# The expert part's output rows: gathered, added by VectorE and scattered plainly, in place of an accumulating scatter

## The reference

```python
g_w, g_idx = lax.top_k(g_prob, 1)                      # one of 4 groups
e_logits = e_logits[jnp.arange(N), g_idx[:, 0]]        # its 8 experts
top_l, top_i = lax.top_k(e_logits, TOP_K_INNER)        # two of them
comb = g_w * jax.nn.softmax(top_l, axis=-1)
eid = g_idx * EXPERTS_PER_GROUP + top_i
...
def expert_block(args):
    xb, e = args
    return (jax.nn.silu(xb @ w_gate[e]) * (xb @ w_up[e])) @ w_down[e]
...
out = jnp.zeros((N, D), jnp.float32).at[stok].add(yp[dest].astype(jnp.float32) * sw[:, None])
# and in decoder_layer:
x = x + hier_moe(hn, ...)
```

## Time and profile before

| | us |
|---|---|
| median of 3 runs | 1002.82 |
| lowest, highest | 997.93, 1004.01 |
| span of the profiled execution | 995.0 |
| busy in it: PE / PEld / DVE / ACT / POOL | 876.9 / 482.7 / 377.6 / 218.1 / 94.0 |

### The profile page before, as it was taken

The page is one execution under the profiler, slowest core; times in us unless marked ns, Lnnn a source line. Parts: engine busy times, 40 slices in busy tenths (PEclk is TensorE's granted clock), DMA queues, the critical chain, the costliest instruction groups (busy, mean ns, idle before and its releaser), DMA issues.

```text
span 995.0 us, 11159 instructions
## 1 busy us (share of the span) xinstructions
PE 876.9 (88%) x4304; PEld 482.7 (49%) x4304; DVE 377.6 (38%) x841; ACT 218.1 (22%) x559; POOL 94.0 (9%) x104
## 2 busy tenths in 40 slices
PE   5999999999999999999969999787786868777774
PEld 4555777777688888745433333222232223222221
DVE  4689687786443445432635112111111111111010
ACT  3532645446332100021211111101010101011110
POOL 0100000000000000011011211101010101010111
PEclk9999999999999999999969999999889999899998
DMA  9621321121122229099289999999999999999994
GB/s 328 207 85 60 110 85 52 43 86 43 43 76 70 74 80 339 14 411 407 99 275 399 397 395 390 397 410 399 398 408 403 416 392 408 408 406 406 408 420 147
DMA packets 35925, 258.56 MB, mean 260 GB/s; under 512 B 9416, under 2 KB 12744, under 8 KB 20744
## 3 DMA queue, kind: packets, MB, share of 16 engines
q1 hardware_dynamic: 28912, 242.19, 61.3%
q0 software_dynamic: 6960, 15.65, 5.5%
HBM read 252.47 MB, written 14.58 MB: 268 GB/s over the span
## 4 chain that ended last, share of the span: by engine, by line
PE 77%; DVE 6%; DMA 6%; issue 6%; another core or an unknown queue 3%; ACT 1%; SPq 1%; POOL 0%; POOLq 0%; DVEq 0%; ACTq 0%
PE ps L1826 24%; PE ps L2111 20%; PE ps L2136 11%; PE ps L1764 6%; PE ps L1985 5%; DMA arena<-in_w_gu 5%; PE ps L2096 1%; PE ps L1911 1%; DMA arena<-in_x 1%; PE ps L1885 1%; PE ps L1842 1%; PE ps L1868 1%; PE ps L2019 1%; PE ps L2112 1%
## 5 line engine op out<-in xcount | busy, mean ns | idle before, releaser
L1826 PE MATMUL ps<-arena 128*128 128x272 f32 x1120 | 266.7, 394 | 2.6 <-DVE arena L1317 1.0
L2111 PE MATMUL ps<-arena 128*64 128x512 f32 x512 | 237.5, 612 | 32.1 <-DMA arena<-in_w_gu 31.2
L2112 PE MATMUL ps<-arena 128*64 128x512 f32 x512 | 237.9, 613 | 0.0
L1826 PEld LDWEIGHTS ps<-arena 128*128 128x128 f32 x1120 | 208.9, 190 | 52.3 <-issue 7.1
L2111 PEld LDWEIGHTS ps<-arena 128*64 128x64 f32 x512 | 67.5, 140 | 172.3 <-issue 137.6
L786 ACT ACTIVATE arena<-ps 128x272 f32<-128x272 f32 (+4 forms) x156 | 71.4, 465 | 345.1 <-PE ps L1826 168.4
L1616 DVE SCALAR_TENSOR_TENSOR arena<-arena,list_w,ps 64x512 f32<-64x512 f32 x32 | 24.0, 749 | 283.0 <-ACT arena L1043 283.0
L2136 PE MATMUL ps<-arena 128*64 128x512 f32 x256 | 67.9, 679 | 26.9 <-issue 26.1
L747 POOL DMA_INDIRECT out_y<-arena,list_i x32 | 45.6, 1426 | 385.8 <-DVE arena L1623 380.0
L2136 PE MATMUL ps<-arena,const 128*64 128x512 f32 x256 | 61.6, 625 | 21.5 <-issue 21.1
L1764 PE MATMUL ps<-arena 128*128 128x512 f32 (+1 forms) x192 | 74.0, 544 | 6.4 <-DVE arena L1109 6.4
(11 more groups left out here) (248 smaller groups left out, 719.8 us busy)
## 6 DMA issues: line engine op xcount, KB each, us to landing
arena<-in_w_gu SPq DMA_DIRECT2D x61, 2048.0 KB, 53.1
arena<-in_w_ed SPq DMA_DIRECT2D x30, 2048.0 KB, 53.5
arena<-in_w_pair SPq DMA_DIRECT2D x20, 1024.0 KB, 4.9
arena<-in_w_gu SPq DMA_DIRECT2D x12, 512.0 KB, 7.6
arena<-in_w_q SPq DMA_DIRECT2D x2, 2048.0 KB, 15.0
arena<-in_w_out SPq DMA_DIRECT2D x2, 2048.0 KB, 12.6
arena<-in_x SPq DMA_DIRECT2D x4, 512.0 KB, 10.0
arena<-in_w_ed SPq DMA_DIRECT2D x2, 1024.0 KB, 7.6
```

Of the source, the lines that this page charges most:

```text
L1826: ins = mm(out, w[:, k, :], tokens[:, k, :], start=k == 0 and q in "127", stop=k == 3, skip_group_check=q not in "127")
L2111: mm(ps[0:C, 2 + s, :], xT[s][:, j, :], w[:, jj, 1, :], start=j == 0, stop=j == JX - 1)
L2112: ins = mm(ps[64:64 + C, 2 + s, :], xT[s][:, j, :], w[:, jj, 0, :], start=j == 0, stop=j == JX - 1)
```

## The change

Each step's 64 rows of y are now gathered into y_rows[s] ahead of time (gather_y, an indirect DMA from y), VectorE adds the down product to both halves in place (add_base), and POOL scatters the sum back by an indirect DMA without compute_op (put_y). add_base waits for the new semaphores y_base[s] (the gathered rows) beside dn_ready. ScalarE's take_y is gone. POOL's loop is written anew: in iteration e it gathers x of e+3, waits until put_y(e-2), the last user of buffer e % 2, has landed, gathers y of e, waits for y_taken e and scatters y of e-1. y_taken is one semaphore now. VectorE's loop is unrolled into 32 straight steps. Overflow items keep the copy and the accumulating scatter (take_y on VectorE alone, add_y).

The diff, without the declarations of the semaphores and the constants of the loop:

```diff
+            def gather_y(index, s):
+                pool.indirect_dma_start(
+                    out=y_rows[s][0:C, :], out_offset=None, in_=o["y"],
+                    in_offset=bass.IndirectOffsetOnAxis(ap=index, axis=0),
+                    bounds_check=T - 1, oob_is_err=False).then_inc(y_base[s], 16)
+
+            def put_y(index, s):
+                pool.indirect_dma_start(
+                    out=o["y"], out_offset=bass.IndirectOffsetOnAxis(ap=index, axis=0),
+                    in_=y_rows[s][0:C, :], in_offset=None,
+                    bounds_check=T - 1, oob_is_err=False).then_inc(y_out[s], 16)
...
-            for e in range(2, NE + 4):
-                if e < NE:
-                    pool.wait_ge(xe_ready, e - 1)
-                    gather_x(list_i[:, e:e + 1], e % 2)
-                if e >= 4:
-                    for q in range(2):
-                        pool.wait_ge(y_taken[q], e - 3)
-                    above(pool, y_out[(e - 1) % 2], 16 * ((e - 3) // 2))
-                    add_y(list_i[:, e - 4:e - 3], e % 2)
+            for e in range(-1, NE + 1):
+                if e + 3 < NE:
+                    pool.wait_ge(xe_ready, e + 2)
+                    gather_x(list_i[:, e + 3:e + 4], (e + 3) % 2)
+                if 0 <= e < NE:
+                    above(pool, y_out[e % 2], 16 * (e // 2))
+                    gather_y(list_i[:, e:e + 1], e % 2)
+                if e > 0:
+                    pool.wait_ge(y_taken, e)
+                    put_y(list_i[:, e - 1:e], (e - 1) % 2)
...
-            def take_y(e, s, turn):
-
-                act.wait_ge(dn_ready, e + 1)
-                above(act, y_out[s], 16 * turn)
-                act.sem_inc(passed, 1)
-                copy(y_rows[s][0:C, 512:1024], ps[64:64 + C, 6 + s, :]).then_inc(y_taken[1], 1)
...
+            def add_base(e, s):
+
+                dve.wait_ge(dn_ready, e + 1)
+                dve.wait_ge(y_base[s], 16 * (e // 2 + 1))
+                dve.sem_inc(passed, 1)
+                tt(y_rows[s][0:C, 0:512], ps[0:C, 6 + s, :], y_rows[s][0:C, 0:512], ALU.add)
+                tt(y_rows[s][0:C, 512:1024], ps[64:64 + C, 6 + s, :], y_rows[s][0:C, 512:1024], ALU.add).then_inc(y_taken, 1)
+
...
-                dve.tensor_copy(y_rows[s][0:C, 0:512], ps[0:C, 6 + s, :]).then_inc(y_taken[0], 1)
...
+            def step(e):
+
+                s = e % 2
+                if e == NE - 1:
+                    add_base(e - 1, 1 - s)
+                hidden(e, s, list_w[0:C, 0, e:e + 1])
+                if e < NE - 1:
                     take_x(e + 1, 1 - s)
-                if not last and (not isinstance(e, int) or e > 0):
-                    take_y(e - 1, 1 - s, half - (1 - s))
+                if 0 < e < NE - 1:
+                    add_base(e - 1, 1 - s)
...
-            for k in range(1, 1 + UNROLL):
-                step(k, k, k // 2)
-            with dve.Fori(1, STEPS) as it:
-                for k in range(1, 1 + UNROLL):
-                    step(it * UNROLL + k, k, it * (UNROLL // 2) + k // 2)
-            step(NE - 1, 1, NE // 2 - 1, last=True)
-            take_y(NE - 1, 1, NE // 2 - 1)
+            for e in range(1, NE):
+                step(e)
+            add_base(NE - 1, 1)
...
-                for q in range(2):
-                    above(pe, y_taken[q], e - 1)
+                above(pe, y_taken, e - 1)
```

More of the change, by code:

```diff
@@ L50 @@
 N_CHUNK = 11
-UNROLL = 10
 MASKED = -1.0e30
@@ L376, in build @@
         dn_ready = sem("dn_ready")
-        y_taken = [sem("y_taken_dve"), sem("y_taken_act")]
+        y_taken = sem("y_taken")
+        y_base = [sem(f"y_base{s}") for s in range(2)]
         y_out = [sem(f"y_out{s}") for s in range(2)]
@@ L386, in build @@
         N_CONST = 6
-        STEPS = (NE - 2) // UNROLL
         def slot(n, *shape):
@@ L777, in _ @@
                     gather_x(item_list_i[:, :], 0)
-                    for q in range(2):
-                        pool.wait_ge(y_taken[q], i + (NE + 1))
-                        pool.sem_inc(passed, 1)
+                    pool.wait_ge(y_taken, i + (NE + 1))
+                    pool.sem_inc(passed, 1)
                     add_y(item_list_i[:, :], 0)
@@ L1058, in _ @@
                 take_hidT(e - 1, 1 - s)
-                if e == NE - 1:
-                    take_y(e - 1, 1 - s, (e - 1) // 2)
                 do_silu(e, s, root_of(e))
-                if e < NE - 1:
-                    take_y(e - 1, 1 - s, (e - 1) // 2)
             take_hidT(NE - 1, 1)
-            take_y(NE - 1, 1, NE // 2 - 1)
             act.wait_ge(item_ready, 1)
@@ L1073, in _ @@
                     take_hidT(i + NE, 0)
-                    take_y(i + NE, 0, i + NE // 2)
         @block.vector
@@ L1617, in hidden @@
                     .then_inc(hid_ready, 1)
+            def add_base(e, s):
[4 more added lines that the diff above has]
+                tt(y_rows[s][0:C, 512:1024], ps[64:64 + C, 6 + s, :], y_rows[s][0:C, 512:1024], ALU.add).then_inc(y_taken, 1)
             def take_y(e, s, turn):
                 dve.wait_ge(dn_ready, e + 1)
-                above(dve, y_out[s], 16 * turn)
+                dve.wait_ge(y_out[s], 16 * turn)
                 dve.sem_inc(passed, 1)
-                dve.tensor_copy(y_rows[s][0:C, 0:512], ps[0:C, 6 + s, :]).then_inc(y_taken[0], 1)
[L1625 to L1631, removed]
-                    take_y(e - 1, 1 - s, half - (1 - s))
-                hidden(e, s, column(list_w, e))
-                if not last:
+                dve.tensor_copy(y_rows[s][0:C, 0:512], ps[0:C, 6 + s, :])
+                dve.tensor_copy(y_rows[s][0:C, 512:1024], ps[64:64 + C, 6 + s, :]).then_inc(y_taken, 1)
+            def step(e):
[4 more added lines that the diff above has]
+                if e < NE - 1:
                     take_x(e + 1, 1 - s)
-                if not last and (not isinstance(e, int) or e > 0):
-                    take_y(e - 1, 1 - s, half - (1 - s))
+                if 0 < e < NE - 1:
+                    add_base(e - 1, 1 - s)
             def list_items():
@@ L1676, in _ @@
             take_x(0, 0)
-            step(0, 0, 0)
+            step(0)
             list_items()
-            for k in range(1, 1 + UNROLL):
-                step(k, k, k // 2)
-            with dve.Fori(1, STEPS) as it:
-                for k in range(1, 1 + UNROLL):
-                    step(it * UNROLL + k, k, it * (UNROLL // 2) + k // 2)
-            step(NE - 1, 1, NE // 2 - 1, last=True)
-            take_y(NE - 1, 1, NE // 2 - 1)
+            for e in range(1, NE):
+                step(e)
+            add_base(NE - 1, 1)
             def list_item(i):
```

## The result

| | before | changed | ratio, 95% interval |
|---|---|---|---|
| median, us | 1001.7 | 1026.4 | 1.0262 [1.0241, 1.0284] |
| span of the profiled execution, us | 995.0 | 1025.5 | |

The change makes the kernel 24.7 us slower. The forecast was 13.4 us slower, 1016.2, with 1000 to 1030 as its range: right in direction and mechanism, short by 11 us in size.

A forecast was written before the change was run, and what follows sets the result against it. The weight DMA stream was taken as the bound. Per expert 0.83 + 0.32 - 0.68 = +0.47 us, times 29 is +13.6, tail -0.2: +13.4 us, so 1002.8 becomes 1016.2, range 1000 to 1030.

The forecast's parts named there:

- The bound: Expert part from 528 us: the weight stream paces it, DMA share 1.01; DMA time taken by other queues lengthens the kernel.
- The plain scatter, 0.32 us: Added put_y, per expert: costs the stream only its bytes, 0.32 us, with the gather's 0.83 as upper bound.
- Rival 3: Added put_y: a plain indirect scatter is as dear as the indirect gather, +28.4 us, 1031; chance 0.16.
- The accumulating scatter, 0.68 us: Removed scatter of y, per expert: costs the stream 0.68 us, about twice its bytes, from windows with scatters alone.
- The y gather, 0.83 us: Added gather_y, per expert: at most the x gather's 0.83 us, found as 1.51 per pair less the scatter.
- The count, 29: Experts whose transfers slow the stream: 29, leaving out the first two or three and the last put; 29 x 0.47 = +13.6 us.
- The tail, -0.2 us: After expert 31: adds +0.85 us, faster landing of the last scatter -1.0, about -0.2 us in sum.
- The chain of waits, no cost: add_base waiting for y_base: 24.3 us against 32.4 in the second stage; up to 2 us late in the first; cost none.
- Rival 2: Even trade: both new transfers cost their bytes, 2 x 0.32 for 0.68 us; 1001.4 us in all; chance 0.28.
- the rule named beside it: A reducing transfer makes two source reads per write, a plain one one; gather plus plain scatter then sums to about nothing.
- The noise: Profiled span 995.0 against median 1002.82: 7.8 us lie outside the span; a measurement tells about 1%, 10 us.

The follow-up runs named there:

- copy_acc: The changed kernel without the y gather, with copies on VectorE in place of the adds and the accumulating scatter as before: 1000.3 us, ratio 0.9996.
- x_halves: The kernel before with its x gather as 128 half rows of 2 KB to 128 partitions: 980.3 us, ratio 0.9804.
- spare_tile128: copy_acc plus one plain, unused DMA in each of 30 steps, 0.131 MB as 1 KB to each of 128 partitions: 1011.7 us, ratio 1.0115.
- spare_spread32: copy_acc plus one plain, unused DMA in each of 30 steps, 32 rows of 4 KB to every fourth partition: 1011.5 us, ratio 1.0113.
- four_buffers: The changed kernel with four y_rows buffers in place of two, so the y gather lands a period earlier: 1027.6 us, ratio 1.0267.
- all_halves: The changed kernel with both gathers and the plain scatter in half rows over 128 partitions and one 128x512 add: 981.2 us, ratio 0.9804.

## Why the prediction was right, and where it was short

**The bound.** Right. The DMA share stayed at 1.01, the period of the second stage grew, and copy_acc shows that everything outside the transfers is free.

**The plain scatter, 0.32 us.** Right: 0.27 us for 0.13 MB alone in a window, 0.28 for the mean size. The ground for it was thin: it leaned on whole-tile transfers, another form. Rival 3, which had it as dear as the gather, falls, though its total of missing weights (1.07 MB per expert) is nearly the measured one (1.04).

**The accumulating scatter, 0.68 us.** Somewhat high. Its difference to the plain one was 0.29 us, not 0.36, and the plain one took 0.28: 0.57. The error came from two lone windows of 9 and 10 us and a scaling.

**The y gather, 0.83 us.** Here is the failed step. It was taken as the most a gather could cost, because the x gather was found so by subtraction from a pair. The runs give 0.95 and 0.96 us, the lone window 0.98. The x gather cost as much: x_halves won 0.64 of it, and a spread transfer still costs 0.29 (spare_tile128, spare_spread32), together 0.93. With 0.57 for the scatter that is 1.50 for the pair, where 1.51 was measured. The pair's sum was right and its split was not, and the change takes away the part that was overrated and adds the one that was underrated. Per expert: 0.95 + 0.28 - 0.57 = +0.66 us in place of +0.47.

**The count, 29.** Too low. Runs price the transfers over all 32 experts: 21.1 us. With the 2.2 us by which the changed kernel's end is longer than copy_acc's that is 23.3, against 26.1 measured between these two and 24.7 between the changed kernel and the one before; 1 to 3 us are not assigned.

**The tail, -0.2 us.** Wrong: it is 2.9 us longer. From the end of the last matmul to the end of the span it is 10.9 us in the kernel before (984.06 to 995.0) and 13.8 in the changed one (1011.69 to 1025.5). The timeline and the landing times of the last scatter of the changed kernel:

```profile
1014.10 0.92 POOL L752 DMA_INDIRECT out_y<-arena,list_i  x1 [10.94 <-DVE arena L1623]
...
DMA to landing us min/median/max: 3.1/8.3/11.8
```

The two adds and the faster landing came as forecast: the last scatter lands at 1017.2, 5.5 us after the last matmul, where it was 6.0. But then 8.3 us pass to the end, and 5.0 passed before. What they are the profile does not say.

**The chain of waits, no cost.** Right: it is late in the first stage only, and four_buffers shows that this is free.

**Rival 2 and the rule named beside it.** By the Trainium skill's page "Collectives: The Full Stack", section "The bandwidth ceiling", a reducing transfer reads twice for each write. The runs agree: 0.57 us for the accumulating scatter, 0.28 for the plain one. The even trade of rival 2 is what all_halves shows (981.2 against 980.3). For the change as it was made it did not decide, since the gather's target cost more than its reads.

**The noise.** The profile of the kernel before belongs to its fastest run (997.9, median 1001.7), so spans differ by 30.5 us where medians differ by 24.7. The forecast put all 7.8 us between that span and the median down to what lies outside the span; for the profiled run itself it is 2.9 (997.9 less 995.0), and the rest is that this run was fast. The shift of 13.4 us does not depend on it. Prices from one profile, multiplied by 30, carry an error of that size.

## What to carry to other kernels

Beside a saturated weight stream, price every small transfer by what the stream loses in the windows around it, not by its bytes or its queue's share: the gather had 5.0% of the engines' time in its window and took three times its bytes from the weights. Give gathers a target on both sides of the 128 partitions (two half rows for each row, one below 64 and one above) even when 64 would do; here that was worth 20 us in the kernel before and 45 us in the changed one. A price found by subtraction bounds nothing: measure the operation alone before it becomes the largest term of a sum.

## What was not expected of the hardware

- 32 rows of 4 KB to 32 neighbouring partitions cost the stream 1.05 us, and to every fourth partition 0.29 us, with the same reads and the same pieces.
- Places of an indirect gather past the bounds check are nearly free: 0.03 us for a DMA of 64 of them, not to be told from nothing.
- Kernels with 30 or 32 more DMAs on queue 0 end later after their last matmul: 13.8 to 14.3 us, 12.2 in all_halves, where copy_acc takes 11.6, x_halves 11.0 and the kernel before 10.9. The cause stays open.
